# Gated DeltaNet scan of a two-layer backbone on one Trainium2 core: products, gates and distances put in another order

## The reference, cut to what matters

```python
decay = exp(where(lower, gc[:, None] - gc[None, :], -inf))
a_strict = where(strict, (k @ k.T) * decay * beta[:, None], 0)
w, u = solve(I + a_strict, [k * (beta * exp(gc))[:, None], v * beta[:, None]])
attn = (q @ k.T) * decay
v_new = u - w @ s
o = (q * exp(gc)[:, None]) @ s + attn @ v_new
s = s * exp(gc[-1]) + (k * exp(gc[-1] - gc)[:, None]).T @ v_new
```

## Time and profile before

| | us |
|---|---|
| median of 3 runs | 4690.57 |
| lowest, highest | 4689.02, 4697.15 |
| the profiled execution, its own time | 4690.96 |
| its span in the trace | 4689.1 |
| mean granted clock of PE over the span | 0.946 of full |

### The profile page before, as it was taken

The page is one execution under the profiler, slowest core; times in us unless marked ns, Lnnn a source line. Parts: engine busy times, 40 slices in busy tenths (PEclk is TensorE's granted clock), DMA queues, the critical chain, the costliest instruction groups (busy, mean ns, idle before and its releaser), DMA issues. The chain is left out here.

```text
span 4689.1 us, 107985 instructions
## 1 busy us (share of the span) xinstructions
PE 4267.7 (91%) x47089; PEld 3821.7 (82%) x47089; DVE 1894.9 (40%) x2829; ACT 1335.9 (28%) x1980; POOL 408.0 (9%) x659
## 2 busy tenths in 40 slices
PE   6999989888969996999998999989898869987998
PEld 5999977787839995889897999978787659976886
DVE  3222236454473436322224222254544474455334
ACT  3211133332252222311113211143322342223222
POOL 1000000332001100010100000000431001100000
PEclk8999999999969998999999999999899879998999
DMA  5232231000200002242423222121001100013332
GB/s 200 81 117 92 92 112 54 19 2 15 61 1 4 4 4 95 72 147 77 162 72 119 70 61 65 54 68 37 15 2 34 42 2 4 4 43 90 98 94 68
DMA packets 344268, 287.36 MB, mean 61 GB/s; under 512 B 9087, under 2 KB 316773, under 8 KB 343397
## 3 DMA queue, kind: packets, MB, share of 16 engines
q1 hardware_dynamic: 326628, 218.92, 15.6%
q0 software_dynamic: 17280, 62.92, 3.9%
HBM read 270.27 MB, written 11.53 MB: 60 GB/s over the span
## 5 line engine op out<-in xcount | busy, mean ns | idle before, releaser
L650 PE MATMUL PS<-x_hi,w_hi 128*128 128x384 f32 (+1 forms) x2464 | 676.7, 344 | 19.1 <-DVE x_lo L554 16.1
L650 PE MATMUL PS<-x_lo,w_hi 128*128 128x384 f32 (+1 forms) x2464 | 675.5, 343 | 0.0
L650 PE MATMUL PS<-x_hi,w_lo 128*128 128x384 f32 (+1 forms) x2464 | 674.4, 343 | 0.0
L650 PEld LDWEIGHTS PS<-x_hi,w_hi 128*128 128x128 f32 x2464 | 449.1, 189 | 40.5 <-issue 26.5
L650 PEld LDWEIGHTS PS<-x_lo,w_hi 128*128 128x128 f32 x2464 | 449.9, 189 | 13.9
L650 PEld LDWEIGHTS PS<-x_hi,w_lo 128*128 128x128 f32 x2464 | 449.2, 188 | 13.9
L783 DVE TENSOR_TENSOR silu_buf<-silu_buf,PS 128x768 f32<-128x768 f32 (+1 forms) x88 | 78.1, 888 | 785.2 <-ACT silu_buf L716 785.2
L626 DVE TENSOR_TENSOR w_lo<-raw_w,w_hi 128x2048 fp32r<-128x2048 f32 x136 | 311.8, 2292 | 131.8 <-ACT w_hi L621 131.8
L694 PE MATMUL PS<-hidden_hi,w_hi 128*128 128x256 f32 (+1 forms) x1232 | 345.6, 351 | 19.6 <-DVE hidden_lo L788 19.6
L621 ACT ACTIVATE w_hi<-raw_w 128x2048 fp32r<-128x2048 f32 x136 | 259.5, 1908 | 337.2 <-PE PS L694 330.1
L694 PE MATMUL PS<-hidden_lo,w_hi 128*128 128x256 f32 (+1 forms) x1232 | 338.2, 345 | 0.0
(11 more groups left out here) (343 smaller groups left out, 7505.5 us busy)
## 6 DMA issues: line engine op xcount, KB each, us to landing
raw_w<-in_ffn_w_dram SPq DMA_DIRECT2D x240, 512.0 KB, 4.4
arena<-in_ada_w_dram POOLq DMA_DIRECT2D x120, 512.0 KB, 6.1
arena<-in_w_in_dram SPq DMA_DIRECT2D x64, 512.0 KB, 3.9
arena<-in_ada_w_dram SPq DMA_DIRECT2D x6, 2048.0 KB, 14.8
raw_w<-in_ffn_w_dram SPq DMA_DIRECT2D x32, 384.0 KB, 3.5
arena<-in_w_out_dram SPq DMA_DIRECT2D x16, 512.0 KB, 3.7
h_save<-arena SPq DMA_DIRECT2D x16, 384.0 KB, 2.3
arena<-h_save SPq DMA_DIRECT2D x2, 3072.0 KB, 9.8
```

What stands on the lines that cost most here:

```text
L650: mm = pe.matmul(PS[:, 4 * b + 2 * g + s, 0:half], w[wo][:, k, g, :], x_split[xo][:, k, a + s * half:a + (s + 1) * half], start=(k == 0 an ...
```

## The change

On PE, the spread of the gates for the next step is made in the last level, between L1357 and L1364; decayed query times state is made there too, before L1357; k times state is made in the head, before the turn of DM; and the head goes by kind of product over both directions, not direction by direction. The turn of DM goes to bank 4g instead of 4g + 3. ACT takes exp of the next step's gates ahead of its copy to AV, splits the exps from the copies, and copies v ahead of k. DVE scales the state as soon as the query products are made, makes the next step's distances right after each direction's output sum, and only then adds to the state and to the output. The split to DMT is now a minimum with a floor mask (0 on and above the diagonal, -10000 below), which takes the place of POOL's masking of the exp (L1251); the attention weights go to DM's place. POOL weights KTOK only once x is ready in both directions, and copies v after both directions' k and q. The last step of the latent loop is taken out of ACT's and DVE's loops, since it has no next step.

Cut to its core:

```diff
+            then(g.memset(upto_floor[:, :], 0.0))
+            then(g.affine_select(out=upto_floor[:, :], in_=upto_floor[:, :], compare_op=ALU.is_ge, fill=-1.0e4, base=0,
                                  pattern=[[1, P]], channel_multiplier=-1))
...
+
+            for first, steps, a, w in dn_loops(layer):
+                ends = first > 0
+                with eng.Fori(0, steps - ends) as i:
+                    step(first, a, w, i, False)
+                if ends:
+                    step(first, a, w, steps - 1, True)
...
-                    pool.wait_ge(dm_ready[g], own + 1)
+                    pool.wait_ge(dm_ready[g], 2 * own + 1)
                 for g in range(2):
+                    pool.wait_ge(x_ready[g], XS * layer + (LEVELS_DN - 1) * (first + i) + 1)
+                for g in range(2):
                     pool.wait_ge(ktok_moved[g], it + 1)
+                    pool.wait_ge(dm_ready[g], 2 * own + 2)
-                    pool.wait_ge(k_decayed[g], own + 1)
-                    gp.tensor_tensor(DMT[g], DMT[g], bc(upto_incl[:, :], 1, [P, DN_H, P]), ALU.mult).then_inc(dm_weighted[g], 1)
...
                     for g in range(2):
-                        c = 4 * g
-                        pe.wait_ge(ug_built[g], it + 1)
-                        pe.matmul(PS[:, c, :], ones[:, :], UG[g].rearrange("p a b -> p (a b)"),
-                                  start=True, stop=True).then_inc(gc_spread[g], 1)
...
+                        product(4 * g + 1, KTc[g], KTc[g]).then_inc(kk_ready[g], 1)
...
+                    for g in range(2):
+                        pe.wait_ge(o_added[g], own + (layer + 1 if g == 0 else 1))
+                        turn(4 * g + 3, KTc[g]).then_inc(ktok_ready[g], 1)
+                    for g in range(2):
+                        pe.wait_ge(ktok_moved[g], it + 1)
+                        product(4 * g + 3, KTc[g], S[g]).then_inc(ks_ready[g], 1)
+                    for g in range(2):
...
+                        pe.wait_ge(vtok_moved[g], it + 1)
+                        turn(4 * g, DM[g]).then_inc(at_turned[g], 1)
...
                             if l == 0:
-                                pe.wait_ge(vtok_moved[g], it + 1)
+                                pe.wait_ge(at_moved[g], it + 1)
                             times(c, 64, lambda u, p: XP[g][p, u, :], lambda u, p: id_c[p]).then_inc(x_turned[g], 1)
-                        if l == 0:
-                            for g in range(2):
-                                pe.wait_ge(s_updated[g], it + 2 * layer + 1)
-                                pe.wait_ge(at_moved[g], it + 1)
-                                for u in range(DN_H):
-                                    mm = pe.matmul(PS[:, 4 * g + 3, u * P:(u + 1) * P], KTc[g][:, u, :], S[g][:, u, :], start=True, stop=True)
-                                mm.then_inc(ks_ready[g], 1)
...
+                    for g in range(2):
+                        pe.wait_ge(kst_ready[g], own + 1)
+                        pe.wait_ge(q_decayed[g], it + 1)
+                        product(4 * g + 3, S[g], QE[g], stop=False).then_inc(so_summed, 1)
...
+                    if first + i < 5:
+                        spread_gates(it + 1)
...
-                        for u in range(DN_H):
-                            mm = pe.matmul(PS[:, c + 2, u * P:(u + 1) * P], KTOK[g][:, u, :], AV[g][:, u, :], start=True, stop=True)
-                        mm.then_inc(s_summed[g], 1)
-                        for u in range(DN_H):
-                            pe.matmul(PS[:, c + 3, u * P:(u + 1) * P], S[g][:, u, :], QE[g][:, u, :], start=True, stop=False)
-                            mm = pe.matmul(PS[:, c + 3, u * P:(u + 1) * P], AV[g][:, u, :], DMT[g][:, u, :], start=False, stop=True)
-                        mm.then_inc(o_summed[g], 1)
+                        product(4 * g + 2, KTOK[g], AV[g]).then_inc(s_summed[g], 1)
+                        product(4 * g + 3, AV[g], ATTN[g], start=False).then_inc(o_summed[g], 1)
...
+            def decays(own, it=None):
+                for g in range(2):
+                    act.wait_ge(gc_spread[g], own + 1)
+                    if it is not None:
+                        act.wait_ge(s_scaled[g], it)
+                        act.wait_ge(q_decayed[g], it)
+                    sc.activation(EB[g], bank(4 * g), ACT.Exp).then_inc(eb_ready[g], 1)
...
-                        act.wait_ge(gc_spread[g], own + 1)
-                        act.wait_ge(s_updated[g], it + 2 * layer + 1)
-                        sc.activation(EB[g], bank(4 * g), ACT.Exp).then_inc(eb_ready[g], 1)
...
+                    if not last:
+                        decays(own + 1, it + 1)
...
+            def distances(g, c):
+                it, own = STEPS * layer + c, 6 * layer + c
+                u = slice(g * DN_H, (g + 1) * DN_H)
+                dve.wait_ge(eb_ready[g], own + 1)
+                v.tensor_tensor(AV[g], bank(4 * g), bc(gcum[:, bass.ds(c, 1), u].rearrange("p o u -> p (o u)"), 2, [P, DN_H, P]),
+                                ALU.subtract).then_inc(dd_ready[g], 1)
+                dve.wait_ge(dd_ready[g], it + 1)
+                v.tensor_scalar(DM[g], AV[g], 0.0, None, ALU.max).then_inc(dd_split[g], 1)
+                v.tensor_tensor(DMT[g], AV[g], bc(upto_floor[:, :], 1, [P, DN_H, P]), ALU.min).then_inc(dd_split[g], 1)
...
-                        dve.wait_ge(dm_weighted[g], 2 * own + 2)
+                        dve.wait_ge(dm_ready[g], 2 * own + 2)
                         dve.wait_ge(kq_ready[g], it + 1)
-                        v.tensor_tensor(DMT[g], DMT[g], bank(4 * g + 2), ALU.mult).then_inc(attn_ready[g], 1)
+                        dve.wait_ge(at_turned[g], it + 1)
+                        v.tensor_tensor(ATTN[g], DMT[g], bank(4 * g + 2), ALU.mult).then_inc(attn_ready[g], 1)
...
                     for g in range(2):
+                        dve.wait_ge(so_summed, 2 * own + g + 1)
+                        v.tensor_tensor(S[g], S[g], EB[g][:, :, P - 1:P].broadcast_to([P, DN_H, P]), ALU.mult).then_inc(s_scaled[g], 1)
+                    for g in range(2):
                         dve.wait_ge(o_summed[g], it + 1)
-                        v.tensor_tensor(S[g], S[g], EB[g][:, :, P - 1:P].broadcast_to([P, DN_H, P]), ALU.mult).then_inc(s_scaled[g], 1)
+                        if not last:
+                            distances(g, first + i + 1)
+                    for g in range(2):
+                        dve.wait_ge(s_scaled[g], it + 1)
+                        v.tensor_tensor(S[g], S[g], bank(4 * g + 2), ALU.add).then_inc(s_updated[g], 1)
...
-                        dve.wait_ge(s_scaled[g], it + 1)
-                        v.tensor_tensor(S[g], S[g], bank(4 * g + 2), ALU.add).then_inc(s_updated[g], 1)
```

More of the change, by code:

```diff
@@ L1276, in times, with spread_gates, turn, product @@
                 return mm
+            def spread_gates(it):
+                for g in range(2):
+                    pe.wait_ge(ug_built[g], it + 1)
+                    pe.matmul(PS[:, 4 * g, :], ones[:, :], UG[g].rearrange("p a b -> p (a b)"),
+                              start=True, stop=True).then_inc(gc_spread[g], 1)
+            def turn(b, t):
+                for u in range(DN_H):
+                    mm = pe.transpose(PS[:, b, u * P:(u + 1) * P], t[:, u, :], ident[:, :])
+                return mm
+            def product(b, lhs, rhs, start=True, stop=True):
+                for u in range(DN_H):
+                    mm = pe.matmul(PS[:, b, u * P:(u + 1) * P], lhs[:, u, :], rhs[:, u, :],
+                                   start=start and (stop or u == 0), stop=stop and (start or u == DN_H - 1))
+                return mm
+            spread_gates(STEPS * layer)
             for first, steps, a, w in dn_loops(layer):
@@ L1384, in act_dn, with step @@
             n = LEVELS_DN - 1
-            for first, steps, a, w in dn_loops(layer):
-                with act.Fori(0, steps) as i:
+            def decays(own, it=None):
[5 more added lines that the diff above has]
+                    sc.activation(EB[g], bank(4 * g), ACT.Exp).then_inc(eb_ready[g], 1)
+            def step(first, a, w, i, last):
                     it, own = STEPS * layer + first + i, 6 * layer + first + i
                     for g in range(2):
-                        act.wait_ge(gc_spread[g], own + 1)
-                        act.wait_ge(s_updated[g], it + 2 * layer + 1)
-                        sc.activation(EB[g], bank(4 * g), ACT.Exp).then_inc(eb_ready[g], 1)
+                        act.wait_ge(dd_split[g], 2 * own + 2)
+                        sc.activation(DM[g], DM[g], ACT.Exp, scale=-1.0).then_inc(dm_ready[g], 1)
+                        sc.activation(DMT[g], DMT[g], ACT.Exp).then_inc(dm_ready[g], 1)
                     for g in range(2):
-                        act.wait_ge(dd_split[g], 2 * own + 2)
-                        sc.activation(DM[g], DM[g], ACT.Exp, scale=-1.0)
```

(15 more changed lines are left out.)

58 lines of the change are left out of this document (16 added, 42 removed).

## The result

The changed kernel takes 4607.65 us (median of 4 runs, 4602.43 to 4612.99), the kernel before, run beside it, 4689.8. The ratio is 0.9825, with a 95% interval from 0.9813 to 0.9836: 82 us faster, where 88 were forecast.

A forecast was written before the change was run, and what follows sets the result against it. No engine is full; a chain through several, turning at the output sum, sets a scan step. Ten steps at 7.4 us (head -8.4, tail +1.0), 12 for first and 2 for last steps give 88: 4690.96 becomes 4603, range 4586 to 4640.

The forecast's parts named there:

- The head: From the last output sum's end to the first level of a step: 10.7 us instead of 19.07, -8.4 us.
- Z: The end of the last output sum, from which the times in the head are counted.
- Minimum at Z + 2.55: DVE's g1 minimum in the head, held by POOL's weighting of DM g0, done 0.75 us later than without POOL.
- K q at Z + 3.3: PE in the head: k q starts then, after waiting for the state, and runs until Z + 5.1.
- K times state at Z + 6.5: PE in the head: k times state twice, after ACT's KTOK, until Z + 8.3, 3.56 us for the four products with the state.
- X ready about Z + 9.0: End of DVE's x chain in the head, 0.72 + 0.89 + 0.42 us for each direction.
- L1451's successor: Last DVE instruction of the x chain, priced 0.42 us with POOL held back, bounds 0.3 and 1.15.
- The tail: From the last level to the output sum, with query products and gate spreads moved in: +1.0 us a step.
- The first step: Head of each layer's first step: first level 6 us earlier, 12 us for two.
- Setup: Two setup instructions on POOL ahead of weight loads: 0.5 us at most, 0 taken.
- first rival: Clock falls in the new head too, with its three groups of transposes: some 4 us a step, 4643 us; chance 0.14.
- third rival: The step becomes bound by PE at the lower clock: 66 us a step, 4955 us; chance 0.03.

The follow-up runs named there:

- no_hold: The changed kernel with POOL's two waits for x taken out, so it weights KTOK as soon as it is there: 4619.28 us, ratio 0.9844.
- fill_before: The kernel before, with PE's idle time in the head filled by throw-away products of k by k: 4694.32 us, ratio 1.0008.

## Why the prediction was right

The time, 4607.65, lies 5 us above the forecast of 4603, inside the range, and the case forecast is the one that came.

- **The head** was to take 10.7 us and takes 10.7 (987.09 to 997.76). Minimum at Z + 2.55: measured 2.6. K q at Z + 3.3: 3.25. K times state at Z + 6.5: 6.4. X ready about Z + 9.0: 8.9.
- **L1451's successor**, bounded by 0.3 and 1.15 us, takes 0.43; the lower price held because POOL stands still then (1.37 in no_hold, where it doesn't).
- **The tail** was sized too small: +1.0 forecast, and 11.5 us from the last level's first product (975.63) to Z, against 9.74: +1.7. The products I had 0.89 us apart leave 1.98 between the first and L1376 where 1.78 were forecast, L1376 takes 1.07, not 0.9, and the spreads 1.83, not 1.70. These three are 0.5 us. That PE loses 0.1 to 0.2 us at each change of the kind of matmul, which my price per instruction left out, is read from these gaps and no run tests it. Another 0.1 is lost ahead of the query products (0.85 us behind 975.63, where 0.75 were forecast) and 0.1 in the last sums (981.36 to 987.09, 5.73 and not 5.60). This is the 0.7 us of 37.29 against 36.6, 7 us in ten steps. Some 3 came back by luck, since the steps before average 44.3 us and not the 44.0 that I priced (1130.66 - 909.14 in five).
- **The first step** was given 6 us; the first level starts 20.1 us into the scan (885.90 - 865.79), not 24.9: 4.8.
- **Setup** was taken as 0 and costs 0.7 us when PE begins. Together: 88 - 7 + 3 - 2.4 for two first steps - 0.7 is 81, and 82 were measured.
- **The clock** stays at 1.00. My first rival had it fall in the new head. The Trainium skill's page TensorE: Matmul & The Clock Gate (Part 4: PE-mode transpose) says that transposes don't count as busy the way matmuls do. With three groups of turns in the head, the clock doesn't fall; since products stand between the turns, this case shows nothing of turns alone.
- **The third rival's mechanism**, the lower clock in the levels, came in an experiment, with a thin stretch just ahead of them. The stretches of two us in the changed head that I looked at (988 to 998) have PE busy for 1.59 or more.

Where the 82 us come from can't be split into a sum: alone, the clock is worth 24 and the port 26, together in the old order less than nothing, and undoing parts of the new order costs 13, 12 and 19 in its place. No run undoes the early spreads and exps alone, or the order by kind of product, so what these give is not shown.

## What to carry to other kernels

Follow one chain through all engines from the point where it turns, and price each part by where it will stand in the new order, since an instruction next to a full engine, a busy port or a low clock has another price. Keep a thin stretch of PE away from the front of its densest one: a lower clock doesn't follow it each time, but where it does, whatever runs next pays. When one engine is full, look at its few remaining waits; moving the additions to the state and one product there gave 14 us more.

## What the runs showed of the hardware

Gaining time at two places made the kernel slower than either alone (4694 against 4664 and 4663), since the idle time went to where the falling clock hits full work. Every fall that these stretches show comes behind a stretch in which PE was little busy, but one and the same gap was followed by a fall in one step or execution and not in another (0.37 busy of 2 us and then 0.52 in the last step of fill_before, 0.32 and then 1.00 in the third; 0.12 and 0.10 busy of 3 us in the feed-forward phase, 1.00 and 0.50 behind). A DVE instruction that gets ahead of POOL at their port only moves the wait to the next one (maximum and minimum took 0.43 and 1.53 us, in the other order the minimum 0.69 and the maximum 1.26). Throw-away work on PE made a kernel 24 us faster.
